# Final norm vector multiplied in early on the last tile, two tiles scaled on GpSimd, result rows laid out residue by residue

## The reference, cut to what matters

```
hn     = x * rsqrt(mean(x^2) + 1e-6) * norm_g
proj   = hn @ w_in                      # 1024 -> 9216: q, k, v, gates, conv inputs
attn   = three dilated window attentions, combined by their softmax denominators
a      = (silu(z_a) * attn) @ w_attn_out
c      = (silu(z_b) * (gb * conv3(gc * hc))) @ w_conv_out
merged = sigmoid(g_a) * a + sigmoid(g_c) * c
h      = x + merged @ w_o
y      = h * rsqrt(mean(h^2) + 1e-6) * final_g      # the part that changes
```

## Time and profile before

| | |
|---|---|
| median of 3 runs | 1471.77 us (1470.95 to 1472.37) |
| the profiled execution | 1471.95 us |
| its span on the slowest core (core 6) | 1470.4 us (all cores: 1465.7 to 1470.4) |
| PE busy | 1451.7 us, 99% of the span |
| DVE, ACT, POOL busy | 60%, 45%, 12% |

### The profile page before, as it was taken

One profiled execution on the slowest core, in us unless ns is written; L12 is line 12 of the kernel. 1 busy time (PEld: TensorE's weight loads), 2 busy tenths in 40 slices (PEclk: granted clock), 3 DMA queues, 4 the chain that ended last, 5 costly groups with the idle time before them and its releaser, 6 DMA issues.

```text
span 1470.4 us, 30492 instructions; the slowest of 8 cores (1465.7 to 1470.4 us)
## 1 busy us (share of the span) xinstructions
PE 1451.7 (99%) x13169; PEld 844.8 (57%) x13213; DVE 885.8 (60%) x1191; ACT 659.9 (45%) x1010; POOL 174.0 (12%) x320
## 2 busy tenths in 40 slices
PE   7999999999999999999999999999999999999998
PEld 5656665655655544444455867877676444444443
DVE  4776473563563995565466458394755967433357
ACT  4576455555555422443232556565655312222234
POOL 3441000000000000122011001000100110000000
PEclk9999999999999999999999999999999999999999
DMA  9864243153154231999395524424341522222158
GB/s 229 206 141 98 59 91 56 20 101 51 25 98 71 38 65 25 170 160 203 53 297 147 116 61 71 89 42 68 73 64 30 86 54 40 34 31 43 23 187 271
DMA packets 114218, 139.21 MB, mean 95 GB/s; under 512 B 73586, under 2 KB 73618, under 8 KB 114084
## 3 DMA queue, kind: packets, MB, share of 16 engines
q0 software_dynamic: 27728, 54.65, 23.3%
q1 hardware_dynamic: 86356, 82.61, 22.6%
HBM read 145.97 MB, written 23.66 MB: 115 GB/s over the span
## 4 chain that ended last, share of the span: by engine, by line
PE 95%; DMA 3%; DVE 1%; issue 0%; ACT 0%; SPq 0%; POOL 0%; DVEq 0%; ACTq 0%; POOLq 0%
PE ps L457 87%; PE ps L469 8%; DMA Y<-xw 3%; PE ps L484 0%; DVE Y L421 0%; SPq L488 0%; ACT Y L408 0%; DVE hnT L445 0%; DVE Y L412 0%; POOL stat L610 0%; DVE Y L445 0%; DVEq L1386 0%; POOL wbf L488 0%; ACT Y L444 0%; ACT hnT L444 0%
## 5 line engine op out<-in xcount | busy, mean ns | idle before, releaser
L457 PE MATMUL ps<-hnT,wbf 128*128 128x512 bf16 (+4 forms) x5648 | 1023.3, 338 | 1.8 <-DMA wbf<-wblk 0.6
L457 PEld LDWEIGHTS ps<-hnT,wbf 128*128 128x128 bf16 x5648 | 522.3, 98 | 442.0 <-DMA wbf<-wblk 1.3
L408 ACT ACTIVATE Y<-ps 128x1024 bf16<-128x1024 f32 (+1 forms) x292 | 240.8, 872 | 193.9 <-PE ps L457 145.2
L444 ACT ACTIVATE Y<-ps 128x512 bf16<-128x512 f32 (+2 forms) x307 | 182.8, 597 | 268.3 <-PE ps L457 246.4
L412 DVE TENSOR_TENSOR Y<-ps,Y 128x512 f32<-128x512 f32 (+1 forms) x196 | 125.8, 674 | 205.0 <-PE ps L469 170.5
L421 DVE SCALAR_TENSOR_TENSOR Y<-Y,ps 128x512 f32<-128x512 f32 x192 | 130.7, 684 | 167.3 <-PE ps L457 142.4
L488 POOL DMA_DIRECT2D wbf<-wblk x160 | 87.8, 549 | 962.9 <-PE ps L457 947.3
L408 ACT ACTIVATE Y<-ps,cf 128x512 f32<-128x512 f32 x128 | 87.3, 685 | 213.6 <-PE ps L457 203.4
L408 ACT ACTIVATE Y<-Y 128x1024 bf16<-128x1024 f32 (+3 forms) x83 | 85.9, 1035 | 122.0 <-DVE Y L421 85.9
L412 DVE TENSOR_TENSOR Y<-Y,et 128x1024 bf16<-128x1024 bf16 x192 | 129.7, 686 | 15.2 <-ACT Y L408 11.0
L469 PEld LDWEIGHTS ps<-Y 64*128 64x128 bf16 x4640 | 114.4, 94 | 31.5 <-issue 26.5
(11 more groups left out here) (48 smaller groups left out, 408.3 us busy)
## 6 DMA issues: line engine op xcount, KB each, us to landing
wbf<-wblk POOLq DMA_DIRECT2D x160, 256.0 KB, 4.8
Y<-xw SPq DMA_DIRECT2D x56, 512.0 KB, 7.4
Y<-xw SPq DMA_DIRECT2D x48, 256.0 KB, 7.0
y<-Y POOLq DMA_DIRECT2D x16, 512.0 KB, 4.1
y<-Y SPq DMA_DIRECT2D x15, 512.0 KB, 6.0
Y<-wblk POOLq DMA_DIRECT2D x16, 256.0 KB, 7.8
et<-etab SPq DMA_DIRECT2D x8, 384.0 KB, 3.6
cv<-Y SPq DMA_DIRECT2D x4, 768.0 KB, 5.2
```

Source lines behind the costliest of these rows:

```text
L408: R.add("act", [lambda e: e.activation(out=out.a, in_=in_.a, func=func, scale=scale, **kw)], c_act(in_.n) + (0.2 if accum is not None else ...
L444: return e.activation(out=out.a, in_=in_.a, func=AF.Copy)
L457: fns = [(lambda e, m=m: e.matmul(m[0].a, lhsT=m[1].a, rhs=m[2].a, start=m[3], stop=m[4])) for m in mms]
```

## The change

Four things are done.

1. Three new buffers `xgV[13]`, `xgV[14]`, `xgV[15]` of 4 KB per partition are named, in space that is free in out1.
2. Tiles 13 and 14 of the second half are finished on POOL. One POOL `TENSOR_TENSOR` multiplies the sum by the final norm vector into `xgV[p]` as soon as the sum is there; a POOL `TENSOR_SCALAR` multiplies by `rs` when that is known; SP then writes `xgV[p]`.
3. For tile 15, DVE multiplies each of the three groups of sums by the final norm vector (`TENSOR_TENSOR`) right behind its sum; the last two instructions then only multiply by `rs` (`TENSOR_SCALAR`).
4. In both halves a tile's 128 result rows stand behind one another in `y`; the host puts them back in token order after the run.

```diff
+        xgV = {13: yb(88, 4096, F32), 14: yb(92, 4096, F32), 15: yb(96, 4096, F32)}
...
         def out_load(h, p):
-            row0 = 16 * own0(h) + R16[p]
+            row0 = R16[p] * (TOK_CORE // 16) + own0(h) - 64
...
+            def scaled_on_pool():
+                xg = xgV[p].cols(0, 1024)
+                ts("pool", xg, xg, rs, None, ALU.mult, cost=1.6)
+                dma("sp", bass.AP(y_d, row0 * D, [[D, 128], [1, D]]), xg.a, [xg], [dram_ref("y", row0)], 1.7)
+
+            if h and p > 12:
+                xg, fg = xgV[p].cols(0, 1024), fgV[h].cols(0, 1024)
+                R.add("pool", [lambda e: e.tensor_tensor(out=xg.a, in0=xt.a, in1=fg.a, op=ALU.mult)], 1.6, [xt, fg], [xg])
+                return scaled_on_pool
+
             def scaled():
                 stt(xt, xt, rs, fgV[h].cols(0, 1024), ALU.mult, ALU.mult)
-                dma("sp" if h else "pool", bass.AP(y_d, (row0 - 1024) * D, [[16 * D, 128], [1, D]]), xt.a, [xt],
+                dma("sp" if h else "pool", bass.AP(y_d, row0 * D, [[D, 128], [1, D]]), xt.a, [xt],
                     [dram_ref("y", row0)], 1.7)
             return scaled
...
-                o, xh = bankv[b].cols(0, n), xb.cols(c0, n)
+                o, xh, xg = bankv[b].cols(0, n), xb.cols(c0, n), xgV[15].cols(c0, n)
...
                 if c0 == 0:
                     waiting[0]()
+                tt(xg, xh, fgV[1].cols(c0, n), ALU.mult)
...
             for nh in range(2):
-                xh = xb.cols(512 * nh, 512)
-                stt(xh, xh, rs, fgV[1].cols(512 * nh, 512), ALU.mult, ALU.mult)
-                dma("sp", bass.AP(y_d, (row0 - 1024) * D + 512 * nh, [[16 * D, 128], [1, 512]]), xh.a, [xh],
+                xg = xgV[15].cols(512 * nh, 512)
+                ts("dve", xg, xg, rs, None, ALU.mult, cost=0.4)
+                dma("sp", bass.AP(y_d, row0 * D + 512 * nh, [[D, 128], [1, 512]]), xg.a, [xg],
                     [dram_ref("y", row0 + nh * TOK_CORE)], 0.9)
```

More of the change, by code:

```diff
@@ L1473 @@
     res = run_bass_kernel_spmd(nc, in_maps, core_ids=list(range(NCORES)))
-    ys = [np.asarray(r["y"], np.float32) for r in res.results]
+    ys = [np.asarray(r["y"], np.float32).reshape(16, -1, D).transpose(1, 0, 2).reshape(-1, D) for r in res.results]
     y_prompt = np.concatenate(ys[0:4], axis=0)[None]
```

## The result

On the same chip the changed kernel took 1482.39 us, the median of five runs (the lowest 1482.06), and the kernel before 1471.64, of five (1470.95 to 1472.37). The ratio is 1.0067, 95% interval 1.0054 to 1.0079, which is 9.9 us slower (7.9 to 11.6); the medians differ by 10.75. The forecast was 1472.9, its range ended at 1475.0. The changed kernel's profiled execution took 1483.14, its span 1481.6 (core 1; the cores from 1475.0 to 1481.6).

A forecast was written before the change was run, and what follows sets the result against it. PE bounds the kernel until the last matmul; only the roughly six microseconds of DVE, ACT and transfers behind it can move. 1471.77 + 1.1 = 1472.9 us, range 1470.3 to 1475.0, called no measurable change.

The forecast's parts named there:

- The sum: Kernel end, followed from tile 13's sum to the last landing: 1471.15 against 1470.04, 1.1 us later.
- POOL, added: New POOL work at the end: twice a product and a scaling of 1024 f32 columns, taken 2.0 and 1.1 us.
- POOL's scaling: One-input scaling of tiles 13 and 14 on POOL: taken 1.1 us, bounds 0.95 to 1.9.
- The product: Two-input POOL product for tiles 13 and 14: taken 2.0 us, bounds 0.95 to 2.8.
- the walk: Instruction-by-instruction schedule of the kernel's end, from tile 13's sum to the last landing: 1.1 us later.
- Who comes first: At tile 13: DVE's scaling 12 holds the path until 1459.67, POOL's product 13 then runs 1459.7 to 1461.7.
- That DVE waits for POOL: At the end: two-input DVE instructions wait for POOL's whole instruction, up to 2.8 us per product.
- PE untouched: Up to the last matmul: no matmul or PE wait added or removed, PE's end stays where it was.
- the layout of `y`: Result writes in the new row order: cost 0, bounds 0.5 us either way at the end.
- the last scalings: Tile 15's last two DVE scalings, now TENSOR_SCALAR: about 0.45 us each, 0.3 from start to start.
- the three last transfers: Transfers of tile 14 and tile 15's halves: issued within 1 us of each other, data one behind the other.
- Rival 3: At the end, slow POOL passes hold the path: 4.2 us slower, 1476.0; chance 0.07.

The follow-up runs named there:

- e3: Kernel before plus a one-column POOL instruction behind the last reciprocal, its result unread: 1477.54 us, ratio 1.0035.
- e4: Kernel before plus the same one-column POOL instruction thirteen microseconds earlier, behind tile 11's statistics: 1472.91 us, ratio 1.0004.
- e6: Kernel before with pairs of POOL and DVE instructions appended behind its last scaling, to time them alone and together; its own time means nothing.
- e2: Kernel before with only the new order of rows in y: 1472.9 us, ratio 1.0003.
- e1: Changed kernel with tiles 13 and 14 scaled on DVE again, early products and new layout kept: 1473.24 us, ratio 1.0005 against the kernel before.
- e5: Changed kernel with only tile 13 finished on POOL, tile 14 scaled on DVE: 1475.61 us, ratio 1.0022 against the kernel before.
- e8: Kernel before with tiles 9 and 10 of the second half finished on POOL: 1473.03 us, ratio 0.9999.
- e9: Changed kernel with only the products of tiles 13 and 14 on POOL, their scalings on DVE: 1483.73 us against 1480.27 for the kernel before, ratio 1.0022.
- e10: Changed kernel run again on another chip: 1488.45 us against 1480.27 for the kernel before, ratio 1.005.

## Why the prediction was wrong

*The step that failed.* "The sum ... to 1470.8, landed at 1471.15. Against 1470.04 that is 1.1 us later." The sum ended at the last landing, because that ended the kernel before. It did not ask what stands behind the last instruction of each engine whose end the change moves. For POOL that is a DRAIN that ends 8.6 us behind its last instruction, and it was in the trace of before, hidden by 93 us of POOL's idleness. Neither "POOL, added" nor the rivals had it; e3 shows it with one column of arithmetic (+5.8 us), e4 that it is free thirteen microseconds earlier. It accounts for 4.7 of the 7.7 us that the forecast tail lacks. The Trainium skill, page "VectorE: DVE Perf Modes", section "The DRAIN you can't avoid", calls the DRAINs ahead of and behind a kernel boilerplate of a constant 12 ns or so, on all five engines. SP's 13 ns agree; POOL's 9112 and 11719 do not.

*A term that was mis-sized.* POOL's scaling: taken 1.1, bounds 0.95 to 1.9, measured 2.86 and 3.09. The reason given, that one read and one write can run side by side, may be so, but the memset beside which it was put does not show the price of the arithmetic; a one-input instruction proved slower than a two-input one, and both bounds were too low. The product, taken 2.0 within 0.95 to 2.8, measured 2.33 to 2.34; the estimate of 2.3 from the page GPSIMD Engine Reference of the Trainium skill, section Elementwise, was the better one. (The page's 4497 ns is for an addition of 2048 f32 columns, not for a product.) Together 5.2 for a tile against the 3.1 taken. The four instructions last 4.4 us more than in the walk; 1.4 of that the walk had as POOL's waits for products 15a and 15b and c, which did not come. So POOL's last end moved from 3.4 us behind the last matmul to 6.46, and this is the other 3.1 us.

*Who comes first.* The walk gave the path to DVE's scaling 12, and POOL's product 13 behind it. In the trace POOL was there 0.02 us earlier, and DVE's scaling took 3.41. That delayed reciprocal 13 and by it POOL's own scaling 13 (1.27 us idle). It cost nothing at the end, though. An estimate: in the walk's order product 13 starts 4.26 us ahead of the last matmul; with the measured 2.34 and 2.86 scaling 13 ends 0.9 behind it, which is where it ended (0.89), and with 2.33, 0.17 and 3.09 behind that POOL is done at 6.5. The walk had the order wrong, and the durations alone made the difference. No run tried the other order.

*That DVE waits for POOL*, taken from symmetry alone: right for the product (e6, 2.27 for 0.69), and DVE's product 15b stretched over POOL's product 14 as foretold (2.51 for two). For the scaling the hold seems to last about 1 us only.

*Right as forecast:* PE untouched, the difference arises behind the last matmul; the layout of `y` worth nothing (e2); the last scalings under 0.5 us each (0.89 for two); the three last transfers issued together (1.63 us for the three), data at 381 GB/s. The gain hoped for from early products is not there even on DVE alone (e1).

*The rivals.* Rival 3, at 0.07, forecast the right sign and a right part of the mechanism (slow POOL instructions that hold the path; product and scaling of together over 4.1). But it gave 1476.0, and its products of 2.8 and scalings of 1.9 were not what came. Without the DRAIN it would have been about right: the span would have been 4.4 us shorter, a tail of some 10.9, 4.4 us over before against its 4.2, in part by luck, its products being too long and its scalings too short. The range was too narrow, since all its ends came from one and the same walk that stopped at the landing.

## What to carry to other kernels

Before work is moved to an engine near the end of a program, look at what the closing line of each engine costs in the trace of before (the DRAIN and the semaphores behind it), and count it from where that engine's last instruction will end. For GpSimd here it was 8.8 us from its last instruction to the end of the span, so its last instruction has to be over that long before the end or not be there. And bound an instruction that no row shows by more than passes over data: a GpSimd scaling was three times the memset of the same size, and whichever of GpSimd and VectorE comes first decides who pays.

## What the runs showed of the hardware, unexpected

- POOL's DRAIN at the program's end ends 8.6 us behind the end of its last arithmetic instruction, for one column as for 1024 (every core of after, e3, e4, e5, e8, e9 and e10). Where POOL's last act was to issue a transfer (before, e1, e2) it is 8.6 on many cores and more on others, up to 9.5 and once 10.7 (before, core 0). ACT's took 0.3 and PE's 2.4. What it does in that time no run shows.
- POOL's one-input f32 scaling of 1024 columns is longer (2.86 us) than its two-input product (2.33), and yet it seems to hold DVE only for about its first microsecond (e6). Why was not tried.
- Single stretches of 3.4 us at the lower clock level (granted 0.50), 16 to 135 us from the start, on none to four cores of an execution, whatever the kernel. In the ten microseconds ahead of one PE had been busy for 6.8 to 8.2 (cores 1, 2 and 5 of after), and for 7.5 at the same place on core 6 of before, where the clock stayed at 1.00. Nothing here shows what brings them on.
